# Attention steps of a fused two-block transformer kernel: two instruction groups change places in ScalarE's and VectorE's programs

## The reference

```python
def block(qi):                                   # one block of 128 queries
    s = jnp.einsum("bqkgd,btkd->bkgqt", qi, k).astype(jnp.float32)
    w = jax.nn.softmax(s, axis=-1).astype(v.dtype)
    return jnp.einsum("bkgqt,btkd->bqkgd", w, v)

y_m = attend(q_m, k_m, v_m) @ lw["w_mo"]         # 8 heads, latent keys and values
y_g = attend(q_g, k_g, v_g) @ lw["w_go"]         # 8 heads over 2 key/value heads
f = jnp.fft.fft2(ug, axes=(1, 3), norm="ortho").real     # 4 groups of 128 columns
g_f, g_m, g_g = jnp.split(jax.nn.sigmoid(gate_logits + lw["b_gate"]), N_BRANCHES, axis=-1)
return (g_f * y_f + g_m * y_m + g_g * y_g) @ lw["w_o"]
```

## Time and profile before

| | |
|---|---|
| time, median of 3 runs | 2835.1 us (2834.52 to 2835.47) |
| profiled execution: its own time | 2834.52 us |
| profiled execution: span | 2832.7 us |
| TensorE matmul busy | 2744.5 us, 97% |
| VectorE, ScalarE, GpSimd busy | 948.2, 1248.7, 1756.6 us |
| mean granted TensorE clock | 0.989 |
| first layer's attention | about 168 to 388 us |
| second layer's attention | about 1045 to 1173 us |

### The profile page before, as it was taken

One profiled execution on the slowest core, in us unless ns is written; L12 is line 12 of the kernel. 1 busy time (PEld: TensorE's weight loads), 2 busy tenths in 40 slices (PEclk: granted clock), 3 DMA queues, 4 the chain that ended last, 5 costly groups with the idle time before them and its releaser, 6 DMA issues.

```text
span 2832.7 us, 48340 instructions
## 1 busy us (share of the span) xinstructions
PE 2744.5 (97%) x19897; PEld 2433.9 (86%) x19897; DVE 948.2 (33%) x1905; ACT 1248.7 (44%) x1667; POOL 1756.6 (62%) x1336
## 2 busy tenths in 40 slices
PE   7999999999999899999999999999999999999999
PEld 5766678768888677898989999999999999989999
DVE  3144431341211534443233223454312314354330
ACT  4335532342322446544444444555434435554443
POOL 1402054434454242687978978558998996757996
PEclk8999999999999999999999999999999999999999
DMA  7554623223323244554545567445555557534553
GB/s 221 139 165 148 209 84 95 90 68 95 100 94 96 55 146 152 165 164 149 194 150 175 181 159 214 125 116 169 187 182 166 186 179 188 166 105 156 179 183 122
DMA packets 401893, 418.93 MB, mean 148 GB/s; under 512 B 78890, under 2 KB 371874, under 8 KB 401423
## 3 DMA queue, kind: packets, MB, share of 16 engines
q1 hardware_dynamic: 401712, 416.37, 47.5%
HBM read 415.27 MB, written 3.16 MB: 148 GB/s over the span
## 4 chain that ended last, share of the span: by engine, by line
PE 87%; DVE 4%; ACT 3%; DMA 2%; POOL 1%; issue 1%; SPq 1%; DVEq 0%; ACTq 0%; POOLq 0%
PE ps L931 31%; PE ps L915 23%; PE ps L899 16%; PE ps L942 15%; PE ps L959 2%; POOL ring_r L1819 1%; DMA ring<-in_w_in 1%; ACT ring_hi L1872 1%; DMA ring<-in_w_ada 1%; ACT arena L2122 1%; DVE hT_r L3192 0%; DVE stat L2943 0%; SPq L583 0%; DMA ring<-in_w_branch_gla 0%; DVE arena L2957 0%
## 5 line engine op out<-in xcount | busy, mean ns | idle before, releaser
L1819 POOL TENSOR_TENSOR ring_r<-ring,ring_hi 128x512 fp32r<-128x512 f32 x1328 | 1754.4, 1356 | 1047.1 <-ACT ring_hi L1872 1019.6
L931 PE MATMUL ps<-hT_r,ring_hi 128*128 128x256 f32 (+1 forms) x5952 | 863.2, 303 | 7.6 <-POOL ring_r L1819 3.4
L931 PEld LDWEIGHTS ps<-hT_r,ring_hi 128*128 128x128 f32 x5952 | 796.2, 191 | 62.2 <-issue 15.6
L1872 ACT ACTIVATE ring_hi<-ring 128x2048 fp32r<-128x2048 f32 x312 | 596.5, 1913 | 427.6 <-DMA ring<-in_ffn_w_down 152.4
L915 PE MATMUL ps<-arena_r,ring_hi 128*128 128x256 f32 (+1 forms) x2784 | 438.8, 303 | 7.3 <-DVE arena L3230 3.1
L942 PE MATMUL ps<-hT_r,ring_r 128*128 128x256 f32 (+1 forms) x2976 | 441.3, 301 | 0.0
L942 PEld LDWEIGHTS ps<-hT_r,ring_r 128*128 128x128 f32 x2976 | 402.2, 190 | 19.6
L915 PEld LDWEIGHTS ps<-arena_r,ring_hi 128*128 128x128 f32 x2784 | 385.7, 191 | 30.6 <-DVE arena L3230 3.9
L915 PE MATMUL ps<-arena_r,ring_r 128*128 128x256 f32 (+1 forms) x1392 | 242.4, 303 | 0.0
L915 PEld LDWEIGHTS ps<-arena_r,ring_r 128*128 128x128 f32 x1392 | 201.7, 191 | 10.3
L899 PE MATMUL ps<-arena 128*64 128x128 f32 (+9 forms) x1616 | 184.5, 340 | 9.6 <-ACT arena L2106 3.2
(11 more groups left out here) (344 smaller groups left out, 2727.5 us busy)
## 6 DMA issues: line engine op xcount, KB each, us to landing
ring<-in_w_in SPq DMA_DIRECT2D x74, 1024.0 KB
ring<-in_w SPq DMA_DIRECT2D x64, 1024.0 KB
ring<-in_w_ada SPq DMA_DIRECT2D x48, 1024.0 KB
ring<-in_ffn_w_up SPq DMA_DIRECT2D x44, 1024.0 KB
ring<-in_ffn_w_gate SPq DMA_DIRECT2D x44, 1024.0 KB
ring<-in_ffn_w_down SPq DMA_DIRECT2D x44, 1024.0 KB
ring<-in_w_in SPq DMA_DIRECT2D x48, 256.0 KB
ring<-in_w_o SPq DMA_DIRECT2D x8, 1024.0 KB
```

The source lines that it names most:

```text
L931: mm = pe.matmul(o, w[0], a[x], start=j == 0 and x == 0, stop=False, skip_group_check=True)
L1819: ins = pool.tensor_tensor(k.ring_lo[s][:, part], k.ring[s][:, part], k.ring_hi[s][:, part], ALU.subtract)
L1872: act.activation(k.ring_hi[s][:, :], k.ring[s][:, :], ACT.Copy).then_inc(k.hi_ready[s], 1)
```

## The change

Two groups of instructions change places; none is added or taken away.

```diff
@@ ScalarE, attention, step u @@
                         tiles = [T.take() for _ in range(2)]
-
-                    def exponentials():
                         act.wait_ge(S["row_max"], T.next("row_max"))
                         for a, (b, v) in enumerate(tiles):
                             act.wait_ge(k.bank_done[b], v)
...
                                 .then_inc(k.bank_read[b], 1)
-
-                    if u < len(todo) and second is None:
-                        exponentials()
                     if u in GROUPS[l]:
                         modulate()
...
                         second = None
                         mixed_in = T.last()
-                        exponentials()
                     if u in dft_steps(l):
@@ VectorE, attention, step u @@
                     if LAG <= u:
                         skip(2)
+                    if u >= 4 and u % 2 == 0:
+                        moved(u - 3)
                     if 1 <= u <= len(todo):
                         probabilities(u - 1)
...
                     if u == 0:
                         skip(1)
-                    if 3 <= u < len(todo) + 1 and u % 2:
-                        moved(u - 2)
                     if second:
```

## The result

The changed kernel takes 2854.7 us (median of 4 runs, 2852.97 to 2857.37) against 2835.3 us beside it: ratio 1.0068, 95% interval 1.0051 to 1.0087. It is slower, as forecast, but by 19.4 us and not by 11.5, and outside the range. The profiled execution took 2854.13 us (span 2852.3).

A forecast was written before the change was run, and what follows sets the result against it. TensorE, busy 97% of the span, was taken as the bound, with late pair copies delaying its flips. Terms of 8.23 us in layer 0 and 3.23 in layer 1 gave +11.5, so 2846.0 us; own range 2843 to 2849, 8-in-10 range 2839.5 to 2849.

The forecast's parts named there:

- Steps 5 and 7 of layer 0: Layer 0: pair copy starts later, behind the late even copy, combining and first-stage copies; +1.57 us each.
- Step 9: Layer 0: pair copy late behind exponentials, even copy and combining, +2.53 us; layer 1: delay hidden by an existing wait, 0.
- Step 17: Layer 0: pair copy goes behind a subtraction on VectorE; +1.17 us.
- Step 19: Layer 0: pair copy goes behind the subtraction, +1.83 us, less a filled panel wait of 0.28, leaving 1.55.
- Step 3: Both layers: first-stage copies without combining, nearly hidden under PV; 0.1 us in all, bounds 0 and 0.4.
- The 0.26 of step 9: Layer 0: earlier exponentials of step 8 give the scores of step 9 their banks sooner; -0.26 us.
- step 5: Layer 1: pair copy late behind exponentials, even copy, combining and first-stage copies; +2.09 us.
- The late rounding: Layer 1: weight panel for step 8 is rounded after step 7's exponentials, so its dense product waits; +0.18 us.
- the port: Layer 1, step 8: VectorE's scaling slowed by GpSimd on their shared port; 0.2 us taken, bounds 0 and 1.82.
- the first rival: Flips wait for something queued behind the pair copy on VectorE, so the change is faster: 2830.8 us; chance 7%.
- The second: Rival: no measurable change, only VectorE's half costs, 5.3 us, giving 2839.8 us; chance 11%.
- The third, the port: Rival: step 8's scaling in layer 1 loses the full 1.82 us to the port, giving 2847.6 us; chance 12%.

The follow-up runs named there:

- the filled kernel: Changed kernel plus dummy TensorE products, their results unread, ahead of the first flip in the stalled steps of both layers; 2847.1 us, ratio 1.0038.
- VectorE's half alone: Kernel before with only VectorE's pair copy moved late, ScalarE's even copy left early; 2843.2 us, ratio 1.0026.
- ScalarE's half: Kernel before with only ScalarE's exponentials moved ahead of the even copy, the pair copy left in place; 2836.2 us, ratio 1.0003.
- the first kernel with dummies in the norms' waits: Kernel before with up to 4, 2 and 12 or 8 more dummy TensorE products in its norms' waits; 2840.1 us, ratio 1.0013.

## Why the prediction missed

The direction, the way the stalls arise and their lengths were right; the range was missed because a whole term was absent. By its own steps:

- Steps 5 and 7 of layer 0, 1.57 each: the waits went from 0.16 to 1.73. Step 9, 2.53: the second flip of step 10 waits 2.47. Step 17, 1.17: 1.32 for 0.16. Step 19, 1.83: 2.12 for 0.23, and the wait of 0.28 for a panel is filled, as is a second one of 0.23 that the prediction left out. Step 3, 0.1: 0.82 for 0.69. The 0.26 of step 9 is gone.
- Layer 1: step 5, 2.09: a wait of 2.03. Step 11, 0.76: 0.83. Step 9, 0: the flip waits 0.76, and the dense product behind it 0.48 for 1.32, so it is hidden. The late rounding, 0.18, and the port, 0.2, are not seen: the dense product of step 8 has no wait, the one of step 9 waits 1.44 for 1.42.
- Layer 0 came to +8.05 us of idle time (8.23 forecast), layer 1 to +2.74 (3.23).
- The step that failed is the sum itself: it took the cost of a stall to be its length, "whatever delays the start of the pair copy by x delays TensorE by x". In layer 0, behind the stalls of steps 6, 8, 10 and 20, TensorE ran at half clock for a while. This added 7.3 us of busy time; the filled kernel is 7.6 us faster than the changed one by the medians. Why it fell behind these and not behind those of step 18 and layer 1 stays open.
- The chances: the first rival (the bank isn't waited for) fell with the late pair copy's 1.57. The second had the right number for VectorE's half alone at step 6, and 2839.8 for 2843.2 us. The third, the port, cost nothing that shows (1.44 us for 1.42).

The trace of before could have warned: the granted clock was 0.51 and 0.50 in the 5 us behind its own waits of 3.19 us at 584 and 959 us, so this kernel does lose clock behind idle time. The prediction speaks of no clock at all.

## What to carry to other kernels

Where TensorE is the bound, price a new stall in two parts: its length, and half clock behind it, here 1.5 to 3.3 us for most stalls of 1.3 to 2.5 us in steps 6, 8, 10 and 20 of layer 0, and sometimes nothing. Profile the same program twice before a difference in the clock is put down to an edit. Look in the profile for where the granted clock already falls, and bound the new cost by those rows. If a stall must stay, dummy products in about half of it kept the clock here; size them by a row, and look behind them for what they move.

## What the runs showed of the hardware

- The granted clock fell behind stalls as short as 1.25 us, and stayed behind others of 2.03 and 2.31 us.
- Two executions of the same program lost clock behind different stalls of the same length (step 20, 2.11 us: 3.21 and 1.94 us for the same 32 products).
- Two orders that alone cost nothing (ScalarE's half) and 7.4 us (VectorE's half) cost 19.4 to 21.4 us together.
- The spread of a kernel's runs follows the clock loosely: over 11 runs of the first kernel with dummies in the norms' waits the fastest (2836.3 us) had a mean clock of 0.993 and the slowest (2843.7 us) 0.990, with 2839.6 us at 0.993 between them.
